# Scores of a retention block by head on 32-row tiles, three input banks, and attention's values side by side

## What is computed

```python
qr = rotary(q_c, pos); kr = rotary(k_c, pos) * HEAD_DIM ** -0.5
inner = einsum('bclhd,bcmhd->bchlm', qc, kc) * decay_mat      # scores of a block, per head
inner = einsum('bchlm,bcmhe->bclhe', inner, vc)
kv    = einsum('bcmhd,bcmhe,hm->bchde', kc, vc, zeta)         # what the block adds to the state
cross = einsum('bclhd,bchde,hl->bclhe', qc, prev, xi)         # what the state gives to the block
...
s = einsum('...lhgd,...mhd->...hglm', q, k) * HEAD_DIM ** -0.5
p = softmax(concat([s, sink]))[..., :-1]
o = einsum('...hglm,...mhd->...lhgd', p, v)                    # the values
```

## Time and profile before

| | |
|---|---|
| median of 3 runs | 1384.29 us |
| profiled execution | 1384.84 us |
| its span | 1382.9 us, so 1.9 us lie around it |
| granted TensorE clock, mean | 0.993 |
| TensorE busy | 1344.9 us, 97% |
| VectorE, ScalarE, GpSimd busy | 667.0, 482.8, 207.1 us |

### The profile page before, as it was taken

How to read it: one execution, slowest core, us unless ns; L and a number is a source line. 1 busy time by engine, 2 the same in 40 slices (tenths; PEclk the granted TensorE clock), 3 DMA queues, 4 the chain that set the end, 5 groups by cost and what they waited for, 6 DMA issues and landing times.

```text
span 1382.9 us, 23798 instructions
## 1 busy us (share of the span) xinstructions
PE 1344.9 (97%) x10254; PEld 1290.8 (93%) x10254; DVE 667.0 (48%) x1158; ACT 482.8 (35%) x994; POOL 207.1 (15%) x243
## 2 busy tenths in 40 slices
PE   8999889999999999999999998999999999999996
PEld 8989859999999999999998896699999999999996
DVE  6555773754444444212458477548444444432113
ACT  5223364652322223322333235556323222232220
POOL 6411113410000000010343021144000000001110
PEclk9999999999999999999999999999999999999998
DMA  4411200222222222222222120021322222222212
GB/s 166 168 47 65 69 1 31 92 92 77 92 77 80 89 77 92 77 88 82 77 107 92 62 73 32 1 77 47 123 77 92 77 84 85 77 92 77 91 47 69
DMA packets 33321, 107.93 MB, mean 78 GB/s; under 512 B 4144, under 2 KB 8640, under 8 KB 33216
## 3 DMA queue, kind: packets, MB, share of 16 engines
q1 hardware_dynamic: 31056, 101.25, 21.2%
q0 software_dynamic: 2160, 5.15, 1.1%
HBM read 103.25 MB, written 3.15 MB: 77 GB/s over the span
## 4 chain that ended last, share of the span: by engine, by line
PE 84%; DVE 10%; issue 2%; ACT 1%; POOL 0%; POOLq 0%; DVEq 0%; ACTq 0%
PE psum L459 26%; PE psum L461 25%; PE psum L460 25%; DVE h_lo L1244 2%; PE psum L751 2%; DVE x L1292 1%; PE psum L479 1%; DVE w_lo L1237 1%; PE psum L556 1%; DVE rsq L1379 1%; PE psum L469 1%; PE psum L580 1%; DVE mx L1488 1%; PE psum L577 1%; DVE prob L1509 0%
## 5 line engine op out<-in xcount | busy, mean ns | idle before, releaser
L459 PE MATMUL psum<-h_hi,w_hi 128*128 128x320 f32 (+1 forms) x2192 | 658.5, 300 | 5.1 <-DVE hid_whole L1281 3.1
L460 PE MATMUL psum<-h_lo,w_hi 128*128 128x320 f32 (+1 forms) x2192 | 649.3, 296 | 0.0
L461 PE MATMUL psum<-h_hi,w_lo 128*128 128x320 f32 (+1 forms) x2192 | 649.2, 296 | 0.0
L459 PEld LDWEIGHTS psum<-h_hi,w_hi 128*128 128x128 f32 x2192 | 415.8, 190 | 12.0 <-issue 4.9
L460 PEld LDWEIGHTS psum<-h_lo,w_hi 128*128 128x128 f32 x2192 | 415.9, 190 | 2.2 <-issue 1.9
L461 PEld LDWEIGHTS psum<-h_hi,w_lo 128*128 128x128 f32 x2192 | 415.8, 190 | 0.0
L1237 DVE TENSOR_TENSOR w_lo<-raw,w_hi 128x1024 fp32r<-128x1024 f32 x184 | 232.3, 1269 | 328.2 <-ACT w_hi L885 328.2
L885 ACT ACTIVATE w_hi<-raw 128x1024 fp32r<-128x1024 f32 x184 | 192.6, 1051 | 179.6 <-DMA raw<-in_wts 179.4
L461 PE MATMUL psum<-hid_hi,w_lo 128*128 128x256 f32 (+1 forms) x672 | 199.6, 297 | 0.0
L460 PE MATMUL psum<-hid_lo,w_hi 128*128 128x256 f32 (+1 forms) x672 | 197.7, 294 | 0.0
L459 PE MATMUL psum<-hid_hi,w_hi 128*128 128x256 f32 (+1 forms) x672 | 197.1, 293 | 0.0
(11 more groups left out here) (179 smaller groups left out, 1115.1 us busy)
## 6 DMA issues: line engine op xcount, KB each, us to landing
raw<-in_wts SPq DMA_DIRECT2D x184, 512.0 KB, 3.2
tab<-in_tabs POOLq DMA_DIRECT2D x2, 642.0 KB, 4.2
x<-in_xT SPq DMA_DIRECT2D x2, 640.0 KB, 10.4
lp<-in_lpar POOLq DMA_DIRECT2D x2, 640.0 KB, 7.0
out_x<-x SPq DMA_DIRECT2D x4, 320.0 KB, 2.3
tab<-in_tabs POOLq DMA_DIRECT2D x2, 577.0 KB, 5.4
x<-in_xT SPq DMA_DIRECT2D x2, 512.0 KB, 5.7
out_x<-x SPq DMA_DIRECT2D x4, 256.0 KB, 2.2
```

Of the source, the lines that this page charges most:

```text
L459: pe.matmul(out, wh, hi, start=first, stop=False)
L460: pe.matmul(out, wh, lo, start=False, stop=False)
L461: return pe.matmul(out, wl, hi, start=False, stop=last)
```

## The change

1. `in_bank` from tile 12 on cycles through banks 0 to 2, so bank 3 is free and tile i waits for the eviction of tile i - 3 where it waited for tile i - 4.
2. The scores of a retention block are eight matmuls in place of two: for each half of the head width and each head, 32 rows of keys against 32 rows of queries, on the 32-row tile of the array at that head's rows, each head into a bank of its own (3 to 6, columns 384 to 511). GpSimd's `qm` with its table goes.
3. One semaphore (`rs_done`, at the end of the scores) stands for three. `kz` and ScalarE's `vtok` copy wait for it, and `inner` waits for the `vtok` copy as well. `ret_in(b)` waits for `inner` of the block before ahead of the transposes.
4. VectorE evicts tiles 12 and 13 right behind the keys' rotation, ahead of `grow_q` and the splits.
5. `values` takes the wide parts of both key heads first and then both half parts.

```diff
 def in_bank(i):
-    return CYCLE[i % len(CYCLE)] if i < 2 * HEAD else (i - 2 * HEAD) % 4
+    return CYCLE[i % len(CYCLE)] if i < 2 * HEAD else (i - 2 * HEAD) % 3
...
                     if b == 0:
                         pe.wait_ge(dve_took, L(2 * HEAD, V_TOOK))
+                        pe.wait_ge(rotq_ready, L(1, 1))
                         pe.wait_ge(rotk_ready, L(1, 1))
                     else:
                         pe.wait_ge(vtok_ready, L(b, NB))
                         pe.wait_ge(kz_ready, L(b, NB))
-                    for bank, row, done in ((5, 2, rk_done), (4, 4, rv_done)):
+                        pe.wait_ge(inner_ready, L(b, NB))
+                    for bank, row in ((5, 2), (4, 4)):
                         for i in (0, 1):
-                            mm = pe.transpose(banks[bank][0:n, i * P:(i + 1) * P], ret[:, row + i, t0:t0 + n],
-                                              ident[:, :])
-                        mm.then_inc(done, 1)
-                    if b:
-                        pe.wait_ge(inner_ready, L(b, NB))
-                    pe.wait_ge(qm_ready, L(b + 1, NB))
-
+                            pe.transpose(banks[bank][0:n, i * P:(i + 1) * P], ret[:, row + i, t0:t0 + n], ident[:, :])
                     for half in (0, 1):
-                        mm = pe.matmul(banks[6][0:n, 0:RET_HEADS * P].rearrange("p (h n) -> p h n", n=P)[:, :, 0:n],
-                                       ret[:, 2 + half, t0:t0 + n], qm[:, b % 2, half, :, 0:n],
-                                       start=half == 0, stop=half == 1)
+                        for hh in range(RET_HEADS):
+                            r = slice(32 * hh, 32 * hh + 32)
+                            mm = pe.matmul(banks[3 + hh][0:n, 3 * P:3 * P + n], ret[r, 2 + half, t0:t0 + n],
+                                           ret[r, half, t0:t0 + n], start=half == 0, stop=half == 1,
+                                           tile_position=(32 * hh, 0))
                     mm.then_inc(rs_done, 1)
...
-                    for h in (0, 1):
-                        out = banks[6 + b % 2][64 * h:64 * h + 64, :].rearrange("p (j n) -> p j n", n=P)
-                        for i, (t, src, n) in enumerate(parts):
+                    for i, (t, src, n) in enumerate(parts):
+                        for h in (0, 1):
+                            out = banks[6 + b % 2][64 * h:64 * h + 64, :].rearrange("p (j n) -> p j n", n=P)
...
                 def vtok_copy(b):
-                    act.wait_ge(rv_done, L(b + 1, NB))
+                    act.wait_ge(rs_done, L(b + 1, NB))
...
-                    dve.wait_ge(rk_done, L(b + 1, NB))
+                    dve.wait_ge(rs_done, L(b + 1, NB))
                     dve.tensor_tensor(kz[0:n, b % 2, :], banks[5][0:n, 0:256],
                                       table("zeta" if b < NB - 1 else "zetas", 256, n), ALU.mult).then_inc(kz_ready, 1)
-                    dve.wait_ge(rs_done, L(b + 1, NB))
-                    dve.tensor_tensor(inner[0:n, b % 2, :, 0:n], grid(b, banks[6][0:n, :], 4),
+                    dve.wait_ge(vtok_ready, L(b + 1, NB))
+                    dve.tensor_tensor(inner[0:n, b % 2, :, 0:n], psum[0:n, 3:7, 3 * P:3 * P + n],
                                       grid(b, table("decay", 512, n), 4), ALU.mult).then_inc(inner_ready, 1)
...
                 rotate(2, 3, ptmp, rotk_ready)
+                in_tile(2 * HEAD)
+                in_tile(2 * HEAD + 1)
                 grow_q()
...
-                pool.wait_ge(rotq_ready, L(1, 1))
-                for b in range(NB):
-                    t0, n = TB[b]
-                    if b >= 2:
-                        pool.wait_ge(rs_done, L(b - 1, NB))
-                    for half in (0, 1):
-                        last = pool.tensor_tensor(qm[:, b % 2, half, :, 0:n],
-                                                  ret[:, half, t0:t0 + n].unsqueeze(1).to_broadcast([P, RET_HEADS, n]),
-                                                  head.to_broadcast([P, RET_HEADS, n]), ALU.mult)
-                    last.then_inc(qm_ready, 1)
```

More of the change, by code:

```diff
@@ L119 @@
 _n = 0
-for _name, _w in (("cos", T), ("sin", T), ("xi", P), ("head", RET_HEADS),
+for _name, _w in (("cos", T), ("sin", T), ("xi", P),
                   ("decay", 4 * P), ("zeta", 2 * P), ("zetas", 2 * P), ("blk", P), ("cdec", 2)):
@@ L266, in program @@
         vk = place("vk", [P, VTILES, P])
-        qm = place("qm", [P, 2, 2, RET_HEADS, P], offset=at[0])
-        qq = place("qq", [P, 4, T], offset=at[0])
-        at[0] += 4 * T * 4
+        qq = place("qq", [P, 4, T])
         st_p = place("st_p", [P, 2, 256])
@@ L329, in program @@
         qxi_ready = sem("qxi_ready")
-        qm_ready = sem("qm_ready")
-        rk_done = sem("rk_done")
-        rv_done = sem("rv_done")
         vtok_ready = sem("vtok_ready")
@@ L1476, in _ @@
                     for g in (0, 1):
-                        in_tile(2 * t + g)
+                        if t > HEAD:
+                            in_tile(2 * t + g)
                         for f in (half_way, more)[g][t]:
@@ L1745, in _ @@
                 firsts = dict(pre=((0, 0), (1, 0)), post=((0, 0), (1, 0)))
-                head = tab[:, TAB["head"]:TAB["head"] + RET_HEADS].unsqueeze(2)
-                pool.wait_ge(rotq_ready, L(1, 1))
-                for b in range(NB):
-                    t0, n = TB[b]
-                    if b >= 2:
-                        pool.wait_ge(rs_done, L(b - 1, NB))
-                    for half in (0, 1):
-                        last = pool.tensor_tensor(qm[:, b % 2, half, :, 0:n],
-                                                  ret[:, half, t0:t0 + n].unsqueeze(1).to_broadcast([P, RET_HEADS, n]),
-                                                  head.to_broadcast([P, RET_HEADS, n]), ALU.mult)
-                    last.then_inc(qm_ready, 1)
                 pool.wait_ge(state_ready, L(NB, NB))
@@ L1831, in constants @@
     cdec = np.exp(logg[of_row][:, None] * np.array([P, DEC], float)[None, :])
-    parts = [cos, sin, xi, of_row[:, None] == np.arange(RET_HEADS)[None, :], decay.reshape(P, -1), zeta(P),
+    parts = [cos, sin, xi, decay.reshape(P, -1), zeta(P),
              np.where(i[:, None] < DEC, zeta(DEC), 0.0), blk, cdec]
```

## The result

The changed kernel takes 1372.9 us (median of 5, 1367.82 to 1374.43) where the one before takes 1384.29: a ratio of 0.9905, 95% interval 0.9887 to 0.9922. It is faster, by 11.4 us where 18.8 were forecast. The time lies 0.1 us inside the upper edge of the range (1360.5 to 1373), and the executions lie 6.6 us apart, while nine of the kernel before, timed beside the experiments, lie within 2.2. The profiled execution happens to be the fastest, 1367.82 us: 17.0 less than the profiled one of before. So there are two things to explain: 1.8 us between the sum (18.8) and what this profile gained, and some 5 us between this profile and the median.

The account below looks back on a forecast made before the run. TensorE was taken to bound the kernel, except where it waits in attention. Retention blocks 9.1, waits 1.1 and attention 8.6 sum to 18.8 us off, giving 1365.5 us against the median of 1384.29; 8-in-10 range 1360.5 to 1373.

Parts of the forecast that it names:

- the sum (18.8): Whole kernel: gains of 9.1 from retention blocks, 1.1 from block 0's waits and 8.6 us from attention.
- Retention blocks: Input stage: scores on four row tiles side by side cut a block from 2.21 to 1.23 us, 9.1 in all.
- in pairs: Rival, retention scores: row tiles share something, scores take 0.87 us, time 1368.8; part of a 0.18 chance.
- one at a time: Rival, retention scores: row tiles queue, scores take 1.74 us, time 1377; chance 0.09 together with several losses.
- drains: Rival, retention scores: every change of row tile drains, block 4.85 us, time 1400; chance of slower 0.03.
- The two waits: Block 0 of each layer: TensorE's waits for ret (0.23 us) and inner (0.33) go, 1.1 us in two layers.
- New waits and three banks: Input stage: the added semaphore waits and tile i waiting for tile i - 3 cost TensorE 0.
- Attention: Chunks 2 to 8: values take 1.15 us instead of 2.30, 4.3 us a layer on the path, 8.6 in all.
- VectorE has no wait: `mx` of chunk 7 begins 1.17 earlier: Attention: with values(2) and (3) shorter, VectorE's 1.09 us wait for h_hi goes; 1.17 of 1.98 us.
- the sign given: End of attention: the first dense record behind values(7) comes 3.1 us closer to the first scores.
- The clock: Rival, attention: with values halved TensorE idles more and stretches at 1.2 GHz cost time; part of a 0.18 chance.
- Both layers: 6.8, time 1372.3: Clock rival's size: a 6.8 us stretch at the end of attention costs 3.4 us per layer; part of 0.18.

Follow-up runs that it names:

- e9: The filled kernel with all sixteen score records of a block on head 0's row tile, same number, size and banks of matmuls: 1379.01 us.
- e6: The filled kernel with GpSimd's ten pairs of 128x512 operations put back, TensorE waiting for them, nothing computed from them: 1370.7 us.
- e5: The filled kernel with evictions of tiles 12 and 13 back behind grow_q and two splits, three banks kept: 1370.85 us.
- the filled kernel: The changed kernel plus four unused fp32 128x128 matmuls ahead of TensorE's wait for prob in chunks 2 to 8: 1368.43 us, again 1368.94 us.
- e7: The filled kernel with only the first of GpSimd's three additions per block of attention's squares: 1366.88 us.
- e0: The changed kernel run again without any edit: 1374.43, 1370.71, 1373.96 and 1373.34 us.
- e2: The changed kernel with the old order of values, key head 0 wide and half, then key head 1: 1374.25 us.
- e3: The changed kernel with four unused 128x128 matmuls ahead of TensorE's wait for prob in chunks 2 to 8: 1368.43 us.
- e8: The filled kernel with six fillers also ahead of the transposes of chunks 0 and 1: 1369.16 us.
- e4: The filled kernel with a block's score matmuls ordered head by head, both halves of a head one after the other: 1367.8 us.

## Why the prediction was right or wrong

**Retention blocks: right, 8 us instead of 9.1.** A block takes 1.35 us where 1.23 was the sum, and the part that was mis-sized is the way back to dense tiles: the first dense record needs 0.26 us to the second instead of 0.15, while the scores and the two changes of shape came out to a hundredth. The kernel before shows this price already, where it comes back from values on 64 rows and columns to dense tiles of 256 columns, 0.23 us from first to second instead of 0.12:

```profile
883.33 0.39 PE L459 MATMUL psum<-h_hi,w_hi 128*128 128x256 f32 x1
883.56 0.28 PE L460 MATMUL psum<-h_lo,w_hi 128*128 128x256 f32 x1
```

The block of 64 was 1.05 against 1.03. So 8 x 0.86 + 2 x 0.62 = 8.1. The choice of four tiles side by side, on rows of 64x64 tiles, was right, and e9 shows that nothing else gives the gain. A block of 1.35 us rules out the rivals "in pairs" (1.5 to 1.6), "one at a time" (2.5) and "drains" (4.9). For the scores the trace has 0.65 us with the change of shape, so 0.50 without it, a factor of 3.4 to the 1.71 of the kernel before. The Trainium skill, TensorE: Matmul & The Clock Gate, section Measured speedup vs the span model, has 3.07, and the estimate by it was 0.56 us: the trace is a little better. Against the same matmuls on one row tile (e9, 1.97 to 0.65 us) it is 3.0.

**The two waits: right, 1.4 us instead of 1.1.** Both are gone. From the last dense record to `ret_out(0)` it is 0.21 us where it was 0.61, so `inner` gave 0.8 in two layers, and block 0 starts 0.6 us earlier in the two together (the record ahead of it is 0.2 us later in layer 0). The prediction added up idle times of 0.23 and 0.33; idle time counts from the modelled end of the record before, and the distance between starts shrank by 0.4 at both places. VectorE's list, walked, was right to within 0.4 us, and e6 shows the cause. What the walk did not count is that the copies also slowed the two splits ahead of the rotation (1.49 and 1.26 us before, 1.21 each after).

**New waits and three banks: right, at nothing.** No wait of TensorE on an eviction in tiles 12 to 35, and e5 shows that the moved eviction is what makes it so.

**Attention: the mechanism right, 7.0 instead of 8.6 at the full clock.** Before, the stage takes 42.5 us at the full clock (layer 1); the filled kernel has it at 38.98, so 3.5 a layer instead of 4.3. Values are 1.17 a chunk, values(7) and (8) give their 2.3. The step that failed is "VectorE has no wait: `mx` of chunk 7 begins 1.17 earlier". Counted from scores(0), in layer 1, it begins 0.27 earlier (23.82 before, 23.55 after), and of the 1.98 us up to the transposes of chunk 8 there came 1.15 (35.27 to 34.12). The prediction took layer 0's wait of 1.09 us for both layers, but that layer had its stretch at half clock just ahead; layer 1 waited 0.63 at the same place:

```profile
868.17 0.49 DVE L1528 TENSOR_TENSOR h_lo<-h_whole,h_hi 128x320 fp32r<-128x320 f32 x1 [0.63 <-ACT h_hi L885]
```

And the wait did not simply go: GpSimd's additions, which begin with ScalarE's `outs`, had begun in VectorE's wait and now begin beside the operation ahead of it: that one and the next take 0.74 us each in place of 0.54 and 0.49. That is 0.45 of the 0.63. e7, where `h_lo` is back at 0.48, shows the cause. So the dense record behind values(7) is 2.3 us closer to the first scores, where 3.1 was the sign given.

**The clock: the rival that came true.** "Both layers: 6.8, time 1372.3" was given as part of 0.18, and it is what the profiled execution of e0 does: two stretches of 10.2 us at 1.2 GHz at the end of attention, 3.6 us dearer in layer 1 than without, in an execution of 1374.4. The mean clocks of four more of the nine executions, 0.983 to 0.985, suggest the same of them. The rival had each stretch at 6.8 us and a cost of half of it; a stretch of 10.2 costs 3.6, since TensorE's last wait for `prob` falls into its first 2 to 3 us. The forecast took the full clock as the likeliest, although it had seen that layer 0 of the kernel before falls to 0.57 in the same stage. The argument missing was where such a fall costs: before, it came at 174.6 us, under VectorE's list, and cost 0.5; with the values halved TensorE idles in every chunk up to the last, and the fall comes where dense work stands behind it. e0, e2 and e3 show cause and size: without halved values the spread is 1.4 us, with the idle time filled the median is 1368.4 and 1368.9.

That the measured time lies inside the range is luck: the forecast took most of its chance for 1360.5 to 1367.5, the median is 0.1 us short of the range's end, and the second set of the same kernel (e0) has 1373.65, outside it.

What stays open is why one execution of the same program falls and another does not, what is left of the spread in e3 and e8, and whether a smaller filler than 0.9 us would do. None of these was tried.

## What to carry to other kernels

Small matmuls on four row tiles, each in a bank of its own, took a third of the time that they took on one (0.65 and 1.97 us for sixteen records), and their order in the list hardly mattered (0.03 us); a change of tile shape is what costs. When TensorE's work is cut in a stage that another engine bounds, look at the clock of the stage behind it: in this kernel halving the values was worth 0.6 us on top of the scores and 5.2 more once the idle time was filled with matmuls that nobody needs. Put such fillers only where the engine idles for longer than they take, at half clock too. An engine that shares nothing with the critical one in the program can still slow it: ask what GpSimd runs beside VectorE's longest list, before and after the change.

## What the runs showed of the hardware

- TensorE starts matmuls of four row tiles within 20 ns of each other (the result), and within 40 ns even if four records of one tile stand in a row in its list (e4): order in the list is not order of start across tiles.
- Going from 128x128 to 32-row tiles, transposes to scores are 0.59 us for four records of 0.11, so 0.15 over; ahead of a matmul of their own shape the same four were 0.49 before the change, so 0.10 of it is the shape. On the way back to 128x128 another 0.11 lies on the second record.
- The granted clock fell to half in stretches of 3.4, 6.8 and 10.2 us, at different places in executions of one program; the mean clock of an execution (0.982 to 0.992) went with its time (1374.4 to 1367.8 us) in the changed kernel. A stretch of 6.8 us early in attention cost 0 to 0.5 us without fillers and 1.5 to 2.0 with them (e3, e5), one of 10.2 at its end 3.6.
- VectorE's 128x576 operation on two SBUF operands takes 0.75 us alone and 1.59 us beside GpSimd's 128x512 products (e6), while evictions out of PSUM kept their 0.88 us for two in the same stretch. GpSimd's product takes 1.04 us beside evictions and 1.55 to 2.02 beside the rotation and the splits.
